# Two-block transformer with a mixture of experts on one core: expert rows fetched by indirect transfers for later pairs, and a reordered opening

## The reference, cut to what matters

```python
mod = (silu_c @ ada_w[layer] + ada_b[layer])          # 6 x 1024 numbers per conditioning vector
sh1, sc1, g1, sh2, sc2, g2 = jnp.split(mod, 6, axis=-1)
h = _rmsnorm(x, norm_w[layer, 0]) * (1.0 + sc1) + sh1  # and the same for ctx
proj = h @ ab_w_in      # q, k, v, gate of 8 retention heads; q, k, v, gate of 8 mLSTM heads; 32 gates
...
# mixture of experts: 8 experts, 2 per token
logits = t @ w_router
top_val, top_idx = lax.top_k(logits, 2); top_w = softmax(top_val)
for e in range(8):
    out = out + combine[:, e:e+1] * ((silu(t @ wg[e]) * (t @ wu[e])) @ w_down[e])
```

## Time and profile before

| | us |
|---|---|
| median of 3 runs | 2336.91 |
| the profiled execution, its own time | 2333.99 |
| its span (first to last instruction) | 2332.2 |
| PE busy in the span | 2236.8 (96%) |
| DVE busy | 1052.4 (45%) |
| ACT busy | 449.4 (19%) |
| POOL busy | 110.2 (5%) |
| DMA moved | 428.13 MB, mean 184 GB/s |

### The profile page before, as it was taken

The page is one execution under the profiler, slowest core; times in us unless marked ns, Lnnn a source line. Parts: engine busy times, 40 slices in busy tenths (PEclk is TensorE's granted clock), DMA queues, the critical chain, the costliest instruction groups (busy, mean ns, idle before and its releaser), DMA issues.

```text
span 2332.2 us, 39035 instructions
## 1 busy us (share of the span) xinstructions
PE 2236.8 (96%) x16791; PEld 1627.1 (70%) x16791; DVE 1052.4 (45%) x2007; ACT 449.4 (19%) x1063; POOL 110.2 (5%) x103
## 2 busy tenths in 40 slices
PE   6989999999999999999999989999999999999997
PEld 4434454478886786678888668888775877777775
DVE  5488465478888335854431454441334520000001
ACT  1310242200000003630000351000332321111101
POOL 0210120000000420000000000000003000000000
PEclk9999999999999999999999999999999899999999
DMA  8424632244554324037885416886534158899994
GB/s 286 161 97 144 214 112 73 72 145 145 174 188 116 97 95 154 1 109 252 293 266 154 150 61 216 288 277 175 189 109 146 46 194 323 301 331 330 331 345 181
DMA packets 306217, 428.13 MB, mean 184 GB/s; under 512 B 11604, under 2 KB 166867, under 8 KB 305803
## 3 DMA queue, kind: packets, MB, share of 16 engines
q1 hardware_dynamic: 303412, 422.55, 53.2%
q10 hardware_dynamic: 2646, 3.26, 0.4%
HBM read 424.55 MB, written 1.13 MB: 183 GB/s over the span
## 4 chain that ended last, share of the span: by engine, by line
PE 90%; DVE 6%; ACT 1%; issue 1%; DMA 1%; ACTq 0%; SPq 0%; DVEq 0%
PE banks L645 76%; PE banks L905 3%; DVE mem L1846 2%; PE banks L654 1%; ACT mem L2871 1%; DVE mem L1849 1%; PE banks L1635 1%; PE banks L1039 1%; PE banks L1459 1%; DVE mem L1842 1%; PE banks L1074 1%; DVE mem L2438 1%; PE banks L1699 1%; PE banks L869 1%; PE banks L1081 0%
## 5 line engine op out<-in xcount | busy, mean ns | idle before, releaser
L645 PE MATMUL banks<-mem 128*32 128x128 f32 (+5 forms) x12722 | 1817.1, 359 | 21.6 <-ACT mem L2871 10.9
L645 PEld LDWEIGHTS banks<-mem 128*128 128x128 f32 (+3 forms) x12722 | 1308.2, 148 | 502.8 <-issue 296.6
L1846 DVE SCALAR_TENSOR_TENSOR mem<-mem 128x512 f32<-128x512 f32 (+4 forms) x523 | 376.9, 746 | 22.1 <-DMA mem<-mem 7.8
L2871 ACT ACTIVATE mem<-banks 128x256 f32<-128x256 f32 (+8 forms) x383 | 152.1, 419 | 1103.1 <-PE banks L645 804.3
L2871 ACT ACTIVATE mem<-mem 128x256 f32<-128x256 f32 (+11 forms) x445 | 192.0, 482 | 662.0 <-DVE mem L1846 469.5
L1849 DVE TENSOR_TENSOR mem<-mem,banks 128x256 f32<-128x256 f32 (+3 forms) x88 | 43.3, 492 | 561.8 <-ACT mem L2871 536.6
L1846 DVE SCALAR_TENSOR_TENSOR mem<-banks,mem 128x256 f32<-128x256 f32 (+7 forms) x258 | 133.6, 543 | 344.8 <-PE banks L645 227.5
L1849 DVE TENSOR_TENSOR mem<-mem 128x256 f32<-128x256 f32 (+13 forms) x272 | 153.5, 576 | 35.2 <-ACT mem L2871 19.8
L1849 DVE TENSOR_TENSOR mem<-banks,mem 128x256 f32<-128x256 f32 (+3 forms) x224 | 90.9, 410 | 101.9 <-PE banks L645 43.9
L654 PE MATMUL banks<-mem 128*128 128x128 f32 (+2 forms) x391 | 61.1, 293 | 24.1 <-DMA mem<-in_ctx 11.3
L654 PEld LDWEIGHTS banks<-mem 128*128 128x128 f32 (+2 forms) x391 | 46.0, 150 | 51.0 <-issue 22.8
(11 more groups left out here) (180 smaller groups left out, 826.6 us busy)
## 6 DMA issues: line engine op xcount, KB each, us to landing
mem<-in_ada_w SPq DMA_DIRECT2D x96, 1024.0 KB, 9.9
mem<-in_moe_w_gate_up SPq DMA_DIRECT2D x64, 1024.0 KB, 10.7
mem<-in_ffn_w_in SPq DMA_DIRECT2D x44, 1024.0 KB, 6.9
mem<-in_moe_w_down SPq DMA_DIRECT2D x48, 768.0 KB, 7.4
mem<-in_moe_w_gate_up SPq DMA_DIRECT2D x32, 768.0 KB, 12.6
mem<-in_ffn_w_out SPq DMA_DIRECT2D x32, 704.0 KB, 6.8
mem<-in_ffn_w_gate_up SPq DMA_DIRECT2D x22, 1024.0 KB, 6.4
mem<-in_ab_w_in SPq DMA_DIRECT2D x16, 1024.0 KB, 9.5
```

The source lines that it names most:

```text
L645: ins = nc.tensor.matmul(o, lhsT, rhs, start=start, stop=stop)
L1846: return V.scalar_tensor_tensor(out=o, in0=a, scalar=sc, in1=b, op0=op0, op1=op1)
L2871: ac = lambda o, i, f, **k: nc.scalar.activation(o, i, f, **k)
```

## The change

Opening: the squares are summed on PE by 128x512 products with a matrix of ones (`sum_squares`), four of them between the transposes, four after the small vectors. ACT squares before it makes the silu, loads the root's table ahead, and takes the root of all 128x512; DVE takes a reciprocal of 128x512, so `norm_sum` and `norm_spread` are gone. The two `ada` panels follow each other. The `ada` panel of n = 2 is removed there and added in n = 7 (`ada_sum` beside, after the second block), and SP's order follows.

Experts: the tokens' rows are also stored to DRAM (`h_rows`, 2 transfers from ACT's queue). For pairs 1 to 3 PE multiplies `pick` by the token numbers (`pair_ids`, 4 one-column products in q = 1 of experts 0, 2, 4), ACT turns the result into integers (`own_ids`), POOL issues two indirect transfers per pair (96 rows of 4 KB each) into `h_tok`, and PE transposes them (`gathered_turned`) where `gather` stood.

```diff
-                for cc in (1024, 2048, 2560, 1536, 3584, 3072):
+                for cc, n in ((1024, 0), (2048, 1), (2560, 1), (1536, 2), (3584, 1), (3072, 2)):
                     plain(w_in, [(cc, 512)])
-                    some_adas(2 if cc == 1536 else 1)
+                    some_adas(n)
...
+            def sum_squares(k):
+                pe.wait_ge(s["norm_squared"], k + 1)
+                last = mm(PS[7][:, :], const("ones"), hT[:, k, :], k == 0, k == 7)
+                if k == 7:
+                    last.then_inc(s["sum_ready"], 1)
+                    c["nsq"].n += KD
...
-            turn_x()
+            turn_x(lambda k: sum_squares(k - 4) if k >= 4 else None)
...
+            for k in range(4, 8):
+                sum_squares(k)
             pe.wait_ge(s["cond_ready"], 4)
-            ada()
-            ada_turned(2, c["ada"].n)
-            norm_sum(T2)
-            ada()
-            ada_turned(3, c["ada"].n)
+            for _ in range(2):
+                ada()
+            for i in (2, 3):
+                ada_turned(i, c["ada"].n - 1)
             if stop >= 1:
-                norm_spread(T2)
...
-                        if n == 5 and b == 1:
+                        if n in (5, 7) and b == 1:
                             ada_sum(2, beside=True)
...
-                    ada_sum(2)
+                    if n != 2:
+                        ada_sum(2)
...
+                def gathered_turned(parts, pair):
+                    pe.wait_ge(s["tokens_gathered"], 32 * pair)
+                    for part in parts:
+                        bank = moved_item()
+                        for b in range(2):
+                            k = part * 2 + b
+                            for j in range(2):
+                                last = turn(bank[:, b * 2 * CAP + j * CAP:b * 2 * CAP + (j + 1) * CAP], h_tok[0:CAP, j, k * P:(k + 1) * P])
+                        last.then_inc(s["moved_ready"], 1)
+                    return c["moved"].n
+                def pair_ids(pair):
+                    await_("picks_ready", "picks")
+                    bank = moved_item()
+                    for j in range(2):
+                        for t in range(2):
+                            last = nc.tensor.matmul(bank[0:CAP, j:j + 1], pick[:, t, j * CAP:(j + 1) * CAP], token_ids[:, t:t + 1],
+                                                    start=t == 0, stop=t == 1)
+                    last.then_inc(s["moved_ready"], 1)
+                    ids_at[pair] = c["moved"].n
...
+                            if q == 1 and e % 2 == 0 and e < NE - 2:
+                                pair_ids(e // 2 + 1)
...
-                            gather((e % 2 * 2,))
+                            gathered_turned((e % 2 * 2,), e // 2 + 1)
...
-            for m in range(8):
-                add_square(m, T2, hT)
+            c["nsq"].n += KD
...
-                norm(0, 0, col("norm_w", 0, 8), 2, between=last_adas)
+                await_("norm_rooted", "sum")
+                V.reciprocal(rstd, rstd)
+                last_adas()
+                dve.wait_ge(s["ada_taken"], c["ada"].n)
+                link(stt(gain, mod[:, 0, 8:16, :], 1.0, col("norm_w", 0, 8).unsqueeze(2).to_broadcast([P, KD, 2]), ALU.add, ALU.mult))
+                for k in range(KD):
+                    for j in range(2):
+                        t = slice(j * L, (j + 1) * L)
+                        stt(hT[:, k, t], xT[:, k, t], gain[:, k, j:j + 1], rstd[:, t], ALU.mult, ALU.mult).then_inc(s["scaled"], 1)
...
-                ada_next()
+                c["panels"].n += 1
                 dve.wait_ge(s["proj_taken"], 9)
...
                     V.tensor_copy(mv[:, t, :], bank[:, :]).then_inc(s["proj_taken"], 1)
+                    if t == 1:
+                        ada_end()
+                        ada_acc(0, 2)
...
+                for t in range(2):
+                    act.dma_start(h_rows[t * P:(t + 1) * P, :], h_tok[:, t, :]).then_inc(s["rows_stored"], 16)
...
+                with pool.If(most <= CAP):
+                    pool.wait_ge(s["rows_stored"], 176 + 32)
+                    for pair in range(1, NE // 2):
+                        pool.wait_ge(s["moved_taken"], ids_at[pair])
+                        for j in range(2):
+                            nc.gpsimd.indirect_dma_start(h_tok[0:CAP, j, :], None, h_rows,
+                                                         bass.IndirectOffsetOnAxis(own_ids[:, j:j + 1], 0)).then_inc(s["tokens_gathered"], 16)
```

More of the change, by code:

```diff
@@ L229, in build @@
             "g_scaled", "g_final_turned", "g_final",
-            "h_passed", "tok_copied", "sum_cleared",
+            "h_passed", "tok_copied", "tokens_gathered", "sum_cleared",
             "blk_tokens", "blk_sums", "blk_act", "blk_copied", "blk_ready", "blk_taken", "blk_silu",
@@ L449, in build @@
         h_own = [v[:, :, L:L + 2 * CAP] for v in (xT, hT)]
+        h_rows = nc.dram_tensor("h_rows", [L, D], F32).ap()
+        own_ids = work(13376, 2, rows=(0, CAP)).bitcast(I32)
+        ids_at = {}
         pick = work(9216, 2, 2 * CAP)
@@ L944, in block_products, with turn_x @@
                     product(e, weights_of(w, 1, 1, q), blk.t4, more=True).then_inc(s["blk_ready"], 1)
-            def turn_x():
+            def turn_x(after):
                 pe.wait_ge(s["x_loaded"], 32)
@@ L1750, in _ @@
                         if more:
-                            gathered = gather((e % 2 * 2 + 1,))
+                            gathered = gathered_turned((e % 2 * 2 + 1,), e // 2 + 1)
                         for m in range(2):
@@ L1920, in last_adas @@
             def last_adas():
-                ada_copied(3)
-                ada_biased(3)
+                for i in (2, 3):
+                    ada_copied(i)
+                for i in (2, 3):
+                    ada_biased(i)
             def norm(par, which, weight, parts, final=False, between=None):
@@ L2167, in _ @@
             V.memset(norm_eps, EPS)
-            V.memset(PS[4][:, 0:P], 0.0)
+            for b in (4, 5):
+                V.memset(PS[b][:, 0:P], 0.0)
             for k in range(8):
@@ L2190, in _ @@
             if stop >= 1:
[L2191 removed]
+                await_("norm_rooted", "sum")
[7 more added lines that the diff above has]
+                        stt(hT[:, k, t], xT[:, k, t], gain[:, k, j:j + 1], rstd[:, t], ALU.mult, ALU.mult).then_inc(s["scaled"], 1)
+                        c["scaled"].next()
                 more = [0]
@@ L2975, in _ @@
             load_vectors(act, 1)
+            squares(T2, hT)
             act.wait_ge(s["packs_copied"], 1)
@@ L2978, in _ @@
                 ac(conds[:, i, :], col(name), ACT.Silu).then_inc(s["cond_ready"], 1)
+            table_of(ACT.Sqrt)
             if stop >= 1:
-                squares(T2, hT)
-                norm_root(4)
+                await_("sum_ready", "norms")
+                ac(rstd, PS[7][:, :], ACT.Sqrt, scale=1.0 / D, bias=norm_eps).then_inc(s["norm_rooted"], 1)
                 act.wait_ge(s["proj_ready"], 1)
@@ L3418, in _ @@
                                 acts_turned(q - 1)
+                            if q == 1 and e % 2 == 0 and e < NE - 2:
+                                ac(own_ids, taken_bank()[0:CAP, 0:2], ACT.Copy).then_inc(s["moved_taken"], 1)
                             if q < 2:
@@ L3533, in _ @@
                     last.then_inc(s["g_diag"], 1)
+            if stop >= 8:
+                pool.wait_ge(s["most_ready"], 1)
+                most = pool.value_load(most_i, min_val=0, max_val=L)
+                with pool.If(most <= CAP):
[5 more added lines that the diff above has]
+                                                         bass.IndirectOffsetOnAxis(own_ids[:, j:j + 1], 0)).then_inc(s["tokens_gathered"], 16)
 def host_constants():
```

22 lines of the change are left out of this document (10 added, 12 removed).

## The result

| | before | after |
|---|---|---|
| median | 2334.06 us (6 runs, 2330.70 to 2337.13) | 2319.81 us (6 runs, 2317.82 to 2324.64) |
| ratio, 95% interval | | 0.9937 [0.9927, 0.9947] |
| profiled execution, its span | 2333.99, 2332.2 | 2319.17, 2317.4 |
| PE busy over the span | 2236.8 | 2224.9 |

The change makes the kernel 0.63% faster: 14.3 us between the medians, 14.8 us between the two profiled executions. The prediction had said 6.1: the right sign, less than half of the size.

A forecast was written before the change was run, and what follows sets the result against it. PE, busy 96% of the span, was taken to bound the kernel. -4.4 - 9.9 + 12.3 - 4.1 = -6.1 gave 2327.9 us profiled, with 2.9 added a median of 2330.8; range 2316 to 2342, forecast band 2325 to 2336.

The forecast's parts named there:

- opening: Start of the kernel: DVE's scaling, which sets the pace there, ends earlier; gain 4.4 us, bounds 1.5 and 6.
- `ada_acc` of n = 2: At n = 2: without this DVE work, PE's 7.25 us wait and the half clock behind it go; gain 9.9 us.
- ring behind n = 7: Before unit 4: panel held longer, so spreads, exponentials and `ret_square(0)` come late and PE idles; loss 12.3 us, bounds 0, 16.
- experts: Six gathering experts: transposes replace gather products, 8.2 us, less 4.1 for `pair_ids`; gain 4.1 us, bounds 2 and 6.
- with a second copy and bias 1.6: Opening: from DVE's copy to the scaling takes 1.6 us, where it took 1.30 before.
- 1.8 to get going: Behind n = 7: start time of the second `ab_w_out` panel, added to 5.3 us for its 2.1 MB.
- a queued transfer saves some of the start: 12.8: Behind n = 7: from the panel's end to the fifth `exp_ctx` takes 12.8 us, against 13.3 from first spread's issue before.
- Rival B: Behind n = 7: spreads hold nothing, as the transfers or `ret_square(0)` come in time; -18.4, 2318.5 us; chance 0.22.
- The new wait: Experts: PE waits on `tokens_gathered`; 16 us are there for POOL's two indirect transfers, so it was taken as hidden.
- Rival C: Experts 0, 2, 4: gathered rows land over 16 us after `own_ids`, 7.5 us each; +16.4, 2353 us; chance 0.10.
- Rival D: Opening and experts give little (1.5 and 2) while the loss behind n = 7 stands; -1.1, 2335.8 us; chance 0.16.

The follow-up runs named there:

- e9: The changed kernel with all eight products of the sum of squares behind the transposes of x instead of four between them: 2323.87 us in a single run.
- e1: The kernel before with only the edits of the opening: 2331.52 us against 2336.21, ratio 0.9982.
- e5: The changed kernel with ScalarE's squares moved ahead, the first before the five exponentials: 2310.53 us, ratio 0.9900 to the kernel before.
- e2: The kernel before with only the `ada_acc` of n = 2 moved to n = 7: 2335.64 us, ratio 0.9994.
- e6: The changed kernel with the five spreads issued ahead of the second `ab_w_out` panel in SyncE's order: 2314.95 us, ratio 0.9911 to the kernel before.
- e7: The changed kernel with each pair's two indirect transfers made twice, the second two after the first landed: 2345.08 us, ratio 1.0047 to the kernel before.

## Why the prediction was right in sign and small in size

| term | predicted | measured | what was off |
|---|---|---|---|
| opening | -4.4 | -6.1 | sum of squares ready 1.0 earlier; 0.6 less from the reciprocal to the scaling |
| `ada_acc` of n = 2 | -9.9 | -10.3 | nothing |
| ring behind n = 7 | +12.3 | +9.6 | the start of the spreads behind the panel |
| experts | -4.1 | -7.8 | one-column records, and the stretch |
| places without an edit | 0 | -0.2 | 1.5 gained before the experts, 1.3 lost at the end |
| sum | -6.1 | -14.8 | |

**Opening: right in mechanism.** The reciprocal took the 3.35 us of its row and ended at 28.35, where I had 29.3, and the clock stayed at 1.00 from 24 on, as said. Of the missing 1.7 us 1.0 is the earlier sum, and that was luck: the input came 0.28 us earlier, and e9, whose transposes took 0.66 less than my row's with the same instructions, has the sum as early, counted from its first transpose, as the changed kernel. 0.6 is the step "with a second copy and bias 1.6", which took 1.0. The scaling took 6.63 with the gain in front of it (0.17), 0.1 longer than before and not 0.4. That the clock held was not certain. In e1 and e5, with the same instructions and the same idle times of 0.90 and 1.48 us in front of the projection, PEclk was 0.50 from 32 to 34, and the projection took 15.67 us instead of 13.97. It cost nothing there, because PE only waited less for DVE behind it (0.72 us instead of 2.42): the sum rests on DVE's chain, as the prediction had it.

**n = 2: right.** No PE row waits for the value copy, the rotations stand at 1.03 and the blocks at 7.03. PE ran into nothing new in n = 7, as said.

**Ring: right in place, chain and order, too large by 2.7.** The first spread came 28.8 us after n = 7 began (predicted about 30), PE stood idle in front of unit 4, released by DVE, that by ACT, that by POOL and DMA. e2 shows that the move alone does this, e5 that ACT's order is what turns the delay into a loss. The panel itself was nearly right, though no row shows the "1.8 to get going": from issue to landing it took 7.7 us (274.53 to 282.3) where the sum had 7.1. The step that failed is "a queued transfer saves some of the start: 12.8", which let the spreads start almost anew behind the panel. The DMA view of the changed kernel around single issues (KB, us to landing) has the panel's second half, issued at 274.94, then the first and the fifth spread, issued at 275.56 and 277.55:

```profile
mem<-in_ab_w_out SPq DMA_DIRECT2D x1, 1024.0 KB, 7.3
mem<-mix_rows SPq DMA_DIRECT2D x1, 384.0 KB, 7.7
mem<-mix_rows SPq DMA_DIRECT2D x1, 384.0 KB, 11.1
```

So the panel has landed at 282.3, the first row 1.0 us behind it (283.3) and the fifth at 288.7. In the kernel before the first row landed 3.6 us after its issue, and in e6, with nothing in the queue, 3.5. POOL and ACT, which before waited 0.2 to 0.6 us at a time for rows, need 8.6 us from the first landing to the end of the fifth exponential instead of 9.7. Together that is 9.6 us from the panel to the fifth exponential (291.88) and not 12.8; from the panel's issue it is 17.35 us where the sum had 19.9. (The queue was not "just empty" at 275.05 either: the same view has the last half panel of the kernel before landing 12.6 us after 264.37, at 277.0.) e6 says the same in another way: taking the panel out of the queue is worth 2.1 us, where the prediction's terms (5.3 + 1.8 - 0.5) give 6.6. The half clock was 2.1 instead of 2.5. Rival B, that the spreads hold nothing, was wrong by e2: 0.9994 where it needed 0.996.

**Experts: right in sign, half of the size.** I took 0.17 us for a record of `pair_ids`, between a transpose and a gather record. Eight one-column records take 0.76 us, 0.095 each, and expose less still: the gain of an even expert is only 0.59 below that of an odd one. That is 2.3 of the 3.7 us. The stretch is 2.59 instead of 2.8, and 4.19 - 2.59 is 1.6 instead of 1.37: 1.4 for six. Both rows that I took the bounds from have 96 columns or more. A row nearer in form stood in the timeline of the opening of the kernel before, and I passed over it:

```profile
27.30 3.57 PE L740 MATMUL banks<-mem 128*128 128x1 f32 x16
```

That is 0.22 for a record of one column at PEclk 0.50; half of it, 0.11, would have been the estimate for full clock.

**The end.** The 1.3 us lost in the last stage are clock again: its 16 transposes took 3.34 us (PEclk 0.73) where they had taken 1.97.

**The new wait: hidden, as taken.** Rival C needed a landing 16 us after `own_ids` and saw 10 to 11. Its price was right: it said 7.5 us for 5 us of lateness, and e7 shows 8.0 for 5.9 on the mean. "DMA: Bandwidth & Descriptors", section "Anatomy of one DMA — SWDGE (gpsimd) path", of the Trainium skill, from which I had estimated 2.9 us for one such transfer, does not agree with this trace: it took 8.4, with the DMA engines busy for 0.94 of the time (1900 to 1912). The 10.7 us row of a 1 MB transfer was the better guide for one in traffic. The rule of the Trainium skill on the shared port ("SBUF — State Buffer", section "SBUF: two separate sides") is neither shown nor refuted here: DVE had 0.7 us of work beside the transfers (1904 to 1914).

**Rival D** (small slips eat the opening and the experts) was wrong in sign: both slips went the other way. The sum came out small because three of its four terms were taken on the careful side (by 1.7, 2.7 and 3.7 us), and errors that point one way don't cancel.

**The time itself.** The forecast was 2325 to 2336 with 2330.8 as its middle, and 2319.8 came out: inside the range of 2316 to 2342, but outside the forecast's own band and within 1.3 us of rival B's 2318.5, whose mechanism is absent. Of the 11.0 us between 2330.8 and 2319.8, 8.7 are the size of the change (14.8 against 6.1). The rest comes from the 2.9 that was added to get from the profiled execution to the median of three runs: with six runs the median of the kernel before is 2334.06, 0.1 above its profiled execution. Who went by the time alone would have taken B for true; only the rows at unit 4, and e2, tell the two apart.

## What to carry to other kernels

In this kernel the transfers that the change delays cost nothing by themselves; they cost 9.6 us because an engine that works in order waits for them with something urgent queued behind. Before moving work that frees a buffer, list what each engine has queued behind the wait for that buffer, and put what the bottleneck needs first. Here moving three lines on ScalarE was worth 9 us, nearly as much as the stall that the change had removed, and nothing where the transfers were on time.

A transfer that waits in a queue does not pay its start again when its turn comes: here the first row landed 1.0 us behind the panel in front of it, against 3.5 from its issue into an empty queue. And consumers that had been waiting for each row catch up when the rows come faster, so a delay at the head of the chain does not reach its end in full.

Single traces of this kernel differ by up to 3 us at places that no edit touches, so a part worth less is told by timed runs or by its own rows, not by the difference of two spans.

## What the runs showed of the hardware

- The lower clock after a gap is not a function of the gap alone. After the same waits (0.18, 0.55 and 1.27 us around four short groups near 1.41 ms) PE went on at full clock in the kernel before and e5 and fell to the lower level in e1, at a price of 2.7 us. In the opening, idle times of 0.90 and 1.48 us left it at 1.00 in the changed kernel and let it fall to 0.50 in e1 and e5, at 1.7 us. At unit 4 a wait of 2.75 us cost no less half clock than one of 8.0 (2.08 and 1.97 us for the first two groups in both; 2.9 and 2.1 us in all).
- GpSimd's indirect transfer of 96 rows of 4 KB holds POOL 0.9 to 1.1 us for the issue and lands 8.4 us later (median of two), both of a pair within 10.0 to 11.1 of the first issue in the three experts of e7; in the changed kernel the DMA engines of the core were busy for 0.94 of 1900 to 1912 us and 0.82 of 1912 to 1930.
- A matmul record of one column with 96 columns of weights takes 0.095 us at full clock.
- A spread of 384 KB landed 3.5 us after its issue into an empty queue (e6), and 1.0 us behind the panel when it was queued behind it (the changed kernel).
- The 36 transposes of x at the start took 5.53 to 6.96 us in runs whose instructions there are the same, with the granted clock at 1.00 in all of them. DVE's copies, one for each block of four transposes, stand 0.85 us apart at first and 0.60 later; the traces differ in when the faster pace begins, and why stays open.
